# One kernel, one schedule line: the first pair's gate matmuls two at a time in every even unit of the attention, none in the odd ones

## What is computed

```python
q, z = jnp.split(h @ w_in, 2, axis=-1)          # q: queries, z: the gate, 1024 channels each
s = jnp.einsum('bqhgd,bkhd->bhgqk', qn, kn) + pos_bias
s = jnp.where(mask, s, NEG_INF)                 # key in the last 128 positions
m = jnp.maximum(jnp.max(s, -1, keepdims=True), sink)
p = jnp.exp(s - m)
p = p / (jnp.sum(p, -1, keepdims=True) + jnp.exp(sink - m))
o = jnp.einsum('bhgqk,bkhd->bqhgd', p, vn)
y = (o * jax.nn.silu(z)) @ w_out
```

## Time and profile before

| | |
|---|---|
| median of 3 runs | 2180.14 us |
| lowest, highest | 2179.26, 2180.89 us |
| the profiled execution's own time | 2178.0 us |
| its span, first to last instruction | 2176.3 us |
| TensorE clock granted, mean over the span | 0.987 |
| PE busy | 2102.6 us (97%) |
| DVE busy | 1225.5 us (56%) |
| ACT busy | 661.5 us (30%) |
| POOL busy | 696.1 us (32%) |
| attention units, first `scores` to last `mix_values` | 1835 to 2010 us of the span |

### The profile page before, as it was taken

The page is one execution under the profiler, slowest core; times in us unless marked ns, Lnnn a source line. Parts: engine busy times, 40 slices in busy tenths (PEclk is TensorE's granted clock), DMA queues, the critical chain, the costliest instruction groups (busy, mean ns, idle before and its releaser), DMA issues.

```text
span 2176.3 us, 24612 instructions
## 1 busy us (share of the span) xinstructions
PE 2102.6 (97%) x9376; PEld 1704.0 (78%) x9376; DVE 1225.5 (56%) x1497; ACT 661.5 (30%) x1134; POOL 696.1 (32%) x378
## 2 busy tenths in 40 slices
PE   7999799899999999999989999999999999999897
PEld 6788687788888888888878888888888778667686
DVE  6999466455545555445684352462572660884555
ACT  6323234321212121212242122122122352786012
POOL 3445634221212121222241121131131321562723
PEclk9999999999999999999999999999999999999998
DMA  4231110522323212232111111111121020010202
GB/s 143 74 107 42 36 49 4 180 80 75 113 99 115 97 53 101 98 114 98 39 49 49 38 59 39 39 58 39 39 78 39 20 78 20 20 40 1 87 10 78
DMA packets 44748, 141.24 MB, mean 65 GB/s; under 512 B 5617, under 2 KB 9857, under 8 KB 44673
## 3 DMA queue, kind: packets, MB, share of 16 engines
q1 hardware_dynamic: 31632, 100.68, 14.5%
q10 hardware_dynamic: 13040, 39.54, 4.9%
HBM read 135.98 MB, written 7.36 MB: 66 GB/s over the span
## 4 chain that ended last, share of the span: by engine, by line
PE 89%; POOL 4%; DVE 3%; ACT 2%; issue 1%; DMA 0%; POOLq 0%; ACTq 0%; DVEq 0%; SPq 0%
PE psum L524 27%; PE psum L526 27%; PE psum L525 27%; POOL temp L410 2%; PE psum L598 1%; PE psum L600 1%; PE psum L599 1%; PE psum L865 1%; POOL w_lo L386 1%; PE psum L876 1%; DVE psum L1411 1%; PE psum L555 1%; PE psum L548 1%; DVE norm_lo L1509 0%; PE psum L844 0%
## 5 line engine op out<-in xcount | busy, mean ns | idle before, releaser
L386 POOL TENSOR_TENSOR w_lo<-w_raw,w_hi 128x1024 fp32r<-128x1024 f32 x174 | 438.9, 2539 | 1123.0 <-ACT w_hi L956 1121.3
L524 PE MATMUL psum<-norm_hi,w_hi 128*128 128x512 f32 x1632 | 638.7, 391 | 11.1 <-ACT temp L1020 11.1
L525 PE MATMUL psum<-norm_lo,w_hi 128*128 128x512 f32 x1632 | 636.8, 390 | 0.0
L526 PE MATMUL psum<-norm_hi,w_lo 128*128 128x512 f32 x1632 | 636.8, 390 | 0.0
L524 PEld LDWEIGHTS psum<-norm_hi,w_hi 128*128 128x128 f32 x1632 | 307.6, 188 | 77.0 <-issue 12.5
L525 PEld LDWEIGHTS psum<-norm_lo,w_hi 128*128 128x128 f32 x1632 | 307.6, 188 | 64.2 <-issue 0.2
L526 PEld LDWEIGHTS psum<-norm_hi,w_lo 128*128 128x128 f32 x1632 | 307.4, 188 | 64.2
L1020 ACT ACTIVATE temp<-psum 128x512 f32<-128x512 f32 x160 | 93.2, 597 | 431.3 <-PE psum L526 411.7
L1470 DVE SCALAR_TENSOR_TENSOR stream<-psum,mods,stream 128x512 f32<-128x512 f32 x160 | 119.8, 750 | 179.1 <-PE psum L526 179.0
L956 ACT CAST w_hi<-w_raw 128x1024 fp32r<-128x1024 f32 x158 | 159.0, 1047 | 122.2 <-PE psum L526 65.2
L1468 DVE TENSOR_TENSOR stream<-psum,stream 128x512 f32<-128x512 f32 x176 | 118.6, 689 | 82.0 <-PE psum L526 81.6
(11 more groups left out here) (195 smaller groups left out, 2958.0 us busy)
## 6 DMA issues: line engine op xcount, KB each, us to landing
w_raw<-in_slabs SPq DMA_DIRECT2D x175, 512.0 KB, 3.5
ada_raw<-in_ada ACTq DMA_DIRECT2D x10, 3072.0 KB, 12.8
stream<-in_x SPq DMA_DIRECT2D x8, 512.0 KB, 9.3
out<-stream SPq DMA_DIRECT2D x8, 512.0 KB, 2.9
skew_scratch<-row_scratch ACTq DMA_DIRECT2D x1, 3072.0 KB, 16.4
ada_raw<-in_ada ACTq DMA_DIRECT2D x1, 2048.0 KB, 9.9
bias<-skew_scratch ACTq DMA_DIRECT2D x4, 512.0 KB, 3.9
c_act<-in_c ACTq DMA_DIRECT2D x1, 512.0 KB, 11.3
```

Source lines behind the costliest of these rows:

```text
L386: nc.gpsimd.tensor_tensor(WL[place][:, :], RAW[at % 2][:, :], WH[place][:, :].bitcast(f32), ALU.subtract).then_inc(slab_ready, 1)
L524: nc.tensor.matmul(dst, wh, xh, start=n == 0, stop=False)
L525: nc.tensor.matmul(dst, wh, xl, start=False, stop=False)
L526: last = nc.tensor.matmul(dst, wl, xh, start=False, stop=n == len(terms) - 1)
```

## The change

In turns 4 to 27 the gate steps `u - 4` and `u - 3` are done in a turn of even `u`, and none in a turn of odd `u`. Turns 28 to 31 stay as they are. No instruction is added or removed; 12 steps are moved one turn ahead.

```diff
                 if 4 <= u < 32:
-                    for n in ((u - 4,) if u < 28 else (2 * u - 32, 2 * u - 31)):
+                    for n in ((u - 4, u - 3) if u % 2 == 0 else ()) if u < 28 else (2 * u - 32, 2 * u - 31):
                         gate_step(n)
```

## The result

The median of 20 runs is 2184.02 us (2181.63 to 2186.83), against 2180.22 us (2177.61 to 2183.20) for 20 runs of the kernel before taken with them. The ratio is 1.0018, with a 95% interval of 1.0011 to 1.0025: slower, by 3.8 us, and under the 0.2% (4.4 us) that the prediction set as the bound. The forecast was 2183.9.

The account below looks back on a forecast made before the run. Two nearly equal loops, PE's own order and mixing, ACT copy, ACT cast, DVE rest, were taken to bound a turn. Terms of 2.94, 0.42, 0.08 and 0.31 added 3.75 us to the 2180.14 median: 2183.9 us, range 2180.8 to 2186.8.

Parts of the forecast that it names:

- The odd turns lose their step: Odd turns of the attention: they keep 4.43 us, PE idling about 0.8 while waiting for data; gain of nothing.
- The even turns get a second step: Full even turns: the second step costs 0.47 to 0.49 us, 4.92 against 4.43; six such turns together 2.94.
- Rival 1: Even turns: the second step costs its full 0.7, 0.2 dearer in each of ten turns, giving 2185.9 us; chance 0.10.
- Turns 4 and 12 are free: Turns 4 and 12: the second step fits into existing slack, in turn 12 from ACT's gate-tile reading; cost 0 each.
- rival 4: Thinner odd turns: PE's clock falls, mixing matmuls run at 0.45 us, 14 us more, about 2198; chance 0.02.
- Turn 16 and turns 20 to 22: Turn 16, with short scores, costs 0.08 us more; turns 20 to 22, with short pieces, 0.31 for the three.
- Turn 6: Turn 6 with two steps: 4.50 us before, 4.92 after, costing 0.42.
- The sum: Whole attention: 2.94 + 0.42 + 0.08 + 0.31 = 3.75 us more.
- The clock behind the attention: After the 11.51 us wait for POOL: the clock's rise may shift, 1.3 us up or down, taken as 0.
- The spread: Whole kernel: within 0.2% chance 0.65, slower 0.32, faster 0.03; counted as no change, close to the edge.

Follow-up runs that it names:

- experiment 1: Kernel before with gate steps k = 1 to 6 of the first pair's first three tiles left out; mark 3 to mark 34 146.59 us against 146.65.
- experiment 6: Kernel before with ACT's casts put ahead of its copy of the mixing, gate reading last; mark 3 to mark 34 143.95 us, 2.70 shorter.
- experiment 8: Changed schedule plus gate reading first and casts ahead of the copy on ACT, against the kernel before; ratio 1.0002, mark 3 to mark 34 146.11 us.
- experiment 3: Kernel before with four gate steps in every fourth turn from 4 to 24, none in others before 28; ratio 1.0039, mark 3 to mark 34 155.17 us.
- experiment 4: Kernel before with the change made in turns 4 and 12 alone, no step in 5 and 13; mark 3 to mark 34 146.66 us against 146.65.
- experiment 5: Kernel before with ACT's reading of a finished gate tile moved to the front of its turn; ratio 0.9994, mark 3 to mark 34 145.66 us.
- experiment 2: Kernel before with two gate steps in every odd turn from 5 to 27, none in even ones; ratio 1.0030, mark 3 to mark 34 151.43 us.
- Experiment 7: Kernel before, one step per turn, with ACT's order reading, casts, copy; 2175.03 us, ratio 0.9978, mark 3 to mark 34 140.84 us.

## Why the prediction was right

- **The odd turns lose their step: gain nothing.** Right. 4.41 to 4.45, and experiment 1 takes the steps out altogether without a gain. The evidence that decided it beforehand was the 0.06 between DVE's end and the mixing; experiments 6 and 8 show from the other side that the turn follows that loop.
- **The even turns get a second step at 0.47 to 0.49.** Right, 0.45 to 0.47: the six plain ones together came to 2.76 where 2.94 was put down. Turn 28, the model for them, takes 4.92, where turns 29 to 31 take 4.89 to 4.90. It was less alike than the prediction has it: ACT reads a gate tile ahead of its casts, so the data come 3.37 behind the mark, just ahead of PE; in a plain even turn they come at 2.87 (turn 14), and the fit is looser. Rival 1, the full 0.7, is refuted by these turns, and experiment 3 shows where that price does hold, from the third step on.
- **Turns 4 and 12 are free.** Right; 4.13 and 4.92, and alone in experiment 4. The reason given for turn 12 is shown by experiment 5. (Rival 1 counts turn 12 among those that would pay 0.2 more, and rival 4 calls the gap there about as large as 0.7 to 0.8; it was 0.41. Neither enters the sum.)
- **Turn 16 and turns 20 to 22.** Forecast 0.08 and 0.31, measured 0.09 and 0.27. Turn 6: forecast 0.42, measured 0.40.
- **The sum.** 3.75 forecast, 3.62 from mark 3 to mark 34, 3.8 between the medians. That 2183.9 is within 0.2 of the median is in part luck: the interval of the ratio allows 2.4 to 5.5 us.
- **The clock behind the attention.** The bound of 1.3 either way was not used: 2.70 for the first six matmuls in both.
- **The spread.** The call "no change, close to the edge of slower" stands; 3.8 us is below 4.4, though 20 runs of each do tell it from nothing.

Left open: what moves mark 3 by up to 5.7 us from execution to execution was not tried. The lower clock goes with it. Added up to mark 3, the time granted 1.2 GHz is 30.7 us in the profiled execution of before, 34.1 and 37.5 in experiments 2 and 8 (mark 3 at 1857.71 and 1856.39), 44.4 in the changed kernel and in experiments 4 to 7 (1857.93 to 1859.59), and 47.8 in experiments 1 and 3 (1860.94 and 1861.28). Whether it is the whole cause, and what sets it, is not shown.

## What to carry to other kernels

An engine that is busy 97% of the time may still be paced by a loop through other engines. To find out, look at the first instruction behind a wait, and see whether it starts when its own predecessor is done or when the releaser is. Work laid into such a wait costs nothing up to the wait's length, so spread it one piece to a wait; gathered into every other one, half of the waits stand empty and the other half overflow. Then look at the order inside the loop: moving one ACT copy, whose reader comes late, behind the casts that start the rest of the loop brought more than any placement of the filler.

## What was not expected of the hardware

How sharp the edge is between a mixing that pays for its first weight load and one that does not. Behind such a wait the second matmul starts 0.34 behind the first, where it is 0.22 to 0.24 in a stream, and the first load (0.19 us) has not run ahead. It is the load that counts and not the wait for data: the gate's first matmul, behind the scores, waits for no other engine, but its load starts together with it too, and it pays the same 0.34 (weight loads and matmuls of before, turn 10):

```profile
1882.96 0.19 PEld L844 LDWEIGHTS psum<-norm_hi,w_hi 128*128 128x128 f32 x1 [0.33 <-issue]
```

```profile
1883.30 0.39 PE L845 MATMUL psum<-norm_lo,w_hi 128*128 128x512 f32 x1
...
1884.19 0.40 PE L525 MATMUL psum<-w_lo,w_hi 128*128 128x512 f32 x1
```

In plain turns of before the rests end 0.02 after PE is free, and the 0.1 is paid in full. In turn 28 they end at 1962.90, and PE is free at about 1963.06. Its load waits for DVE too (weight loads and matmuls of before, turn 28), and yet the mixing pays nothing:

```profile
1962.95 0.19 PEld L524 LDWEIGHTS psum<-w_hi 128*128 128x128 f32 x1 [0.15 <-DVE w_lo L1870]
```

```profile
1962.83 0.40 PE L846 MATMUL psum<-norm_hi,w_lo 128*128 128x512 f32 x1
1963.07 0.40 PE L524 MATMUL psum<-w_hi 128*128 128x512 f32 x1
1963.30 0.40 PE L525 MATMUL psum<-w_lo,w_hi 128*128 128x512 f32 x1
```

So between data 0.02 late and data 0.16 early lies a difference of about 0.2 for the turn. Experiment 7 shows its two parts: of the 0.21 that a plain turn gained (4.43 to 4.22), 0.09 is the time before the mixing (0.32 to 0.23) and 0.10 the gap behind its first matmul (0.34 to 0.24).
